# Expert pairs of a decoder step: the next pair's gather inside the down products, a smaller form, another order of pairs

## The reference, cut to what matters

```
logits = h @ w_router + b_router                  # 264 tokens, 8 experts
probs  = softmax(logits)
top_p, top_e = top_k(probs, 2);  top_p /= sum(top_p)
for each token and each of its two experts e:
    out[token] += top_p * ((silu(h @ w_gate[e]) * (h @ w_up[e])) @ w_down[e])
x = x + g_f * out
y = rmsnorm(x, norm_out)
```

## Time and profile before

| | |
|---|---|
| median of three runs | 1342.48 us |
| the profiled execution's own time | 1343.16 us |
| its span, first to last instruction | 1341.3 us |
| PE busy | 1277.4 us (95%) |
| weights and other data read from HBM | 458.94 MB |
| granted TensorE clock, mean | 0.988 |

### The profile page before, as it was taken

How to read it: one execution, slowest core, us unless ns; L and a number is a source line. 1 busy time by engine, 2 the same in 40 slices (tenths; PEclk the granted TensorE clock), 3 DMA queues, 4 the chain that set the end, 5 groups by cost and what they waited for, 6 DMA issues and landing times.

```text
span 1341.3 us, 28791 instructions
## 1 busy us (share of the span) xinstructions
PE 1277.4 (95%) x12903; PEld 746.0 (56%) x12904; DVE 219.8 (16%) x597; ACT 124.5 (9%) x247; POOL 36.1 (3%) x125
## 2 busy tenths in 40 slices
PE   7999999999998699999899999999999999999995
PEld 3777788877885433346565534665343555343553
DVE  0299200000005601010110201002010002010002
ACT  2201310000002310000001000001000001000002
POOL 1000100000003200000000000000000000000000
PEclk9899999999999899999999999999999999999998
DMA  9999575556436299999999899999999999999993
GB/s 334 408 402 387 202 277 201 211 174 231 162 121 251 90 406 417 418 420 423 420 407 352 356 365 423 392 381 420 417 418 420 422 419 417 419 418 418 423 419 121
DMA packets 87885, 462.23 MB, mean 345 GB/s; under 512 B 8747, under 2 KB 12119, under 8 KB 52663
## 3 DMA queue, kind: packets, MB, share of 16 engines
q1 hardware_dynamic: 85937, 456.41, 85.1%
q10 hardware_dynamic: 1814, 3.85, 0.8%
HBM read 458.94 MB, written 2.24 MB: 344 GB/s over the span
## 4 chain that ended last, share of the span: by engine, by line
PE 80%; DMA 13%; DVE 2%; issue 2%; POOL 1%; ACT 1%; SPq 0%; DVEq 0%; ACTq 0%; POOLq 0%
PE bank L1624 36%; PE bank L1389 25%; DMA ring<-in_w_exp_down_dram 13%; PE bank L1646 9%; PE bank L1572 2%; PE bank L1358 2%; PE bank L1678 1%; PE bank L1595 1%; PE bank L1286 1%; POOL ROWS L625 1%; SPq L527 0%; DVE xT L957 0%; ACT MIX L890 0%; PE bank L1516 0%; PE bank L1337 0%
## 5 line engine op out<-in xcount | busy, mean ns | idle before, releaser
L1624 PE MATMUL bank<-ring,HT 128*32 128x512 f32 (+1 forms) x5376 | 510.1, 539 | 3.5 <-DMA ring<-in_w_exp_up_dram 3.5
L1624 PEld LDWEIGHTS bank<-ring,HT 128*32 128x32 f32 x5376 | 189.1, 110 | 312.5 <-issue 298.2
L1389 PE MATMUL bank<-HT,ring 128*128 128x264 f32 x1024 | 234.0, 390 | 2.5 <-POOL HT L619 2.5
L1389 PEld LDWEIGHTS bank<-HT,ring 128*128 128x128 f32 x1024 | 195.4, 192 | 43.6 <-issue 10.3
L1646 PE MATMUL bank<-ring,hid_t 128*32 128x256 f32 x2560 | 149.2, 379 | 2.6 <-DMA ring<-in_w_exp_down_dram 2.6
L1646 PEld LDWEIGHTS bank<-ring,hid_t 128*32 128x32 f32 x2560 | 86.2, 110 | 56.3 <-issue 5.6
L1389 PE MATMUL bank<-BIG,ring 128*128 128x264 f32 x480 | 107.3, 386 | 0.0
L1389 PEld LDWEIGHTS bank<-BIG,ring 128*128 128x128 f32 x480 | 91.1, 190 | 15.5
L1646 PE MATMUL bank<-ring,COND 128*32 128x256 f32 x1568 | 89.6, 380 | 9.9 <-DMA ring<-in_w_exp_down_dram 9.7
L1646 PEld LDWEIGHTS bank<-ring,COND 128*32 128x32 f32 x1568 | 50.2, 110 | 47.8 <-DMA ring<-in_w_exp_down_dram 18.5
L1223 DVE TENSOR_TENSOR hid_t<-bank,hid_t 128x512 f32<-128x512 f32 (+1 forms) x22 | 14.2, 643 | 361.0 <-PE bank L1624 360.3
(11 more groups left out here) (230 smaller groups left out, 527.8 us busy)
## 6 DMA issues: line engine op xcount, KB each, us to landing
ring<-in_w_exp_gate_dram SPq DMA_DIRECT2D x64, 1024.0 KB, 15.1
ring<-in_w_exp_up_dram SPq DMA_DIRECT2D x64, 1024.0 KB, 16.2
ring<-in_w_exp_down_dram SPq DMA_DIRECT2D x64, 1024.0 KB, 24.1
ring<-in_w_ada_dram SPq DMA_DIRECT2D x48, 1024.0 KB, 12.9
ring<-in_w_exp_gate_dram SPq DMA_DIRECT2D x64, 768.0 KB, 16.0
ring<-in_w_exp_up_dram SPq DMA_DIRECT2D x64, 768.0 KB, 14.6
ring<-in_w_exp_down_dram SPq DMA_DIRECT2D x32, 1536.0 KB, 25.2
ring<-in_w_in_dram SPq DMA_DIRECT2D x10, 1024.0 KB, 24.9
```

The costliest lines, as they stand in the source:

```text
L1389: ins = t_.matmul(banks_of[label][:, 0:NT], w[:, k, f * P:(f + 1) * P], src(k0 + k), start=(k0 + k == 0), stop=(k0 + k == k_tiles - 1))
L1624: ins = t_.matmul(bank[GATE_BANKS[role][g]][i * GRP:(i + 1) * GRP, 0:cols], xg[:, k, c0:c0 + GRP], w[:, i, :], start=(k == 0), stop=(k == ...
```

## The change

A fourth form, thin (3 large groups and 1 small), takes the value 0. The ranks of the pairs become (0,6), (1,7), (2,4), (3,5); before they were (0,4), (1,7), (2,5), (3,6). The gather of pair p+1 moves into the down products of pair p: two of its four banks in the large half 0, ahead of the loads 1 and 2, two in the small half 1, ahead of the loads 8 and 10. It uses the banks 3 to 6 and always computes all 224 columns. The first gather stands in front of the loop, and DVE makes its pick matrices and the copy of `pmT` ahead of the flags. The last pair gathers as well, for a pair that does not follow. The store and the spread of `pmT` move from ACT's to POOL's DMA queue.

```diff
-VARIANTS = (("narrow", (3, 2)), ("slim", (5, 1)), ("mid", (5, 2)))
-SLIM = 2
-RANK_AT = (0, 4, 1, 7, 2, 5, 3, 6)
+VARIANTS = (("narrow", (3, 2)), ("slim", (5, 1)), ("thin", (3, 1)), ("mid", (5, 2)))
+THIN, SLIM = 0, 2
+RANK_AT = (0, 6, 1, 7, 2, 4, 3, 5)
...
-GATHER_BANKS = (0, 1, 2, 3)
+GATHER_BANKS = (3, 4, 5, 6)
...
             with nc.body(f"{tag}_not_slim", valid_engines=[kind]):
+                eng.br_eq(form, THIN, on_true=f"{tag}_thin", on_false=f"{tag}_not_thin")
+            with nc.body(f"{tag}_not_thin", valid_engines=[kind]):
                 eng.br_lt(form, SLIM, on_true=f"{tag}_narrow", on_false=f"{tag}_mid")
...
+            pool.wait_ge(on("pmT_ready"), 1)
+            pool.dma_start(pm_rows, pmT[:]).then_inc(on("pm_rows_stored"), 16)
...
             def pair_scalar(p, j, groups):
-                take_batch(p, groups)
...
+                take_batch(p + 1)
                 act.wait_ge(on("large_out_done"), p + 1)
...
+            act.wait_ge(on("new_stored"), 6 * 16)
+            take_batch(0)
             act.wait_ge(on("flags_ready"), 1)
...
             dve.wait_ge(on("pm_ready"), 1)
+            v.tensor_copy(pos_tab[:, :, 0:NE], pm_sorted[:, :, 0:NE])
...
+            dve.wait_ge(on("slots_ready"), 1)
+            pick_matrix(0)
+            empty("turned", v.tensor_copy(pmT[:], wait_bank("turned")[0:2 * NE, 0:NT]))
+            landed("turned")
+            dve.sem_inc(on("pmT_ready"), 1)
             link(v.tensor_tensor(moved[:, 0:2], keys[:].unsqueeze(2).to_broadcast([P, 2, NE, NE]),
...
+            def gather(p, i):
+
+                b = GATHER_BANKS[i]
+                for half in range(2):
+                    d = 2 * i + half
+                    for t in range(3):
+                        ins = t_.matmul(bank[b][:, half * BOTH:(half + 1) * BOTH], h_rows[:, t, d * P:(d + 1) * P],
+                                        pick[t], start=(half == 0 and t == 0), stop=(t == 2), skip_group_check=True)
+                ins.then_inc(on("gathered"), 1)
+
+            pe.wait_ge(on("pick_ready"), 1)
             for bk in range(7):
                 pe.wait_ge(emptied[bk], bank_total[bk])
+            for i in range(len(GATHER_BANKS)):
+                gather(0, i)
             pe.wait_ge(on("flags_ready"), 1)
...
-                gather(p, groups)
...
-                down("large", 0, {4: [("small", 1, g) for g in range(count["small"])]})
-                down("small", 0, {})
+                pe.wait_ge(on("pick_ready"), p + 2)
+                down("large", 0, {4: [("small", 1, g) for g in range(count["small"])]}, {1: 0, 2: 1})
+                down("small", 0, {}, {8: 2, 10: 3})
                 down("large", 1, {})
                 down("small", 1, {})
 
+                pe.wait_ge(on("xg_ready"), p * 4 + 8)
```

More of the change, by code:

```diff
@@ L660, in _ @@
             g.tensor_copy(slot_row, slot_row.bitcast(I32)).then_inc(on("slots_ready"), 1)
+            pool.wait_ge(on("pmT_ready"), 1)
+            pool.dma_start(pm_rows, pmT[:]).then_inc(on("pm_rows_stored"), 16)
+            pool.wait_ge(on("pm_rows_stored"), 16)
+            for i, dst in enumerate((posb, wgtb)):
+                spread = pm_rows[i * NE:(i + 1) * NE, :].rearrange("e n -> (e n)").unsqueeze(0)
+                pool.dma_start(dst.rearrange("p e n -> p (e n)"),
+                              spread.to_broadcast([P, NE * NT])).then_inc(on("tables_spread"), 16)
         @block.scalar
@@ L835, in _, with take_batch @@
             rows(2)
-            def take_batch(p, groups):
-                here = slice(columns_of("large", groups[0] - 1), columns_of("small", groups[1]))
-                for b in GATHER_BANKS:
-                    act.wait_ge(on("gathered"), p * 4 + (b + 1))
-                    src = bank[b][:, 0:2 * BOTH].rearrange("p (t n) -> p t n", t=2)[:, :, here]
-                    a.activation(xg[:, 2 * b:2 * b + 2, here], src, ACT.Copy).then_inc(on("xg_ready"), 1)
+            def take_batch(p):
+                for i, b in enumerate(GATHER_BANKS):
+                    act.wait_ge(on("gathered"), p * 4 + (i + 1))
+                    src = bank[b][:, 0:2 * BOTH].rearrange("p (t n) -> p t n", t=2)
+                    a.activation(xg[:, 2 * i:2 * i + 2, :], src, ACT.Copy).then_inc(on("xg_ready"), 1)
             def pair_scalar(p, j, groups):
-                take_batch(p, groups)
                 for s in range(2):
@@ L1201, in _ @@
             dve.sem_inc(on("pmT_ready"), 1)
+            link(v.tensor_tensor(moved[:, 0:2], keys[:].unsqueeze(2).to_broadcast([P, 2, NE, NE]),
+                                 order.unsqueeze(1).to_broadcast([P, 2, NE, NE]), ALU.mult))
+            link(v.tensor_reduce(sorted_keys[:], moved[:, 0:2], AX_X, ALU.add))
+            v.tensor_copy(excess[:, 0, :], sorted_keys[:, 1, :])
+            link(v.tensor_tensor(excess[:, 1, :], sorted_keys[:, 1, :], caps[:], ALU.subtract))
+            link(v.tensor_reduce(stat[:, 0:1], excess[:, 1, :], AX_X, ALU.max))
+            link(v.tensor_tensor(excess[:], excess[:], fits[:].unsqueeze(1).to_broadcast([P, 2, NE]), ALU.is_gt))
+            link(v.tensor_tensor(excess[:], excess[:], forms[:].unsqueeze(1).to_broadcast([P, 2, NE]), ALU.mult))
+            v.tensor_reduce(flag_f[:, 0:NE].rearrange("p (a j) -> p a j", a=2),
+                            excess[:].rearrange("p a (j r) -> p a j r", r=2), AX_X, ALU.add)
+            v.tensor_copy(flag_f[:, NE:2 * NE], sorted_keys[:, 0, :])
+            link(v.tensor_scalar(flag_f[:, 2 * NE:2 * NE + 1], stat[:, 0:1], 0.0, 1.0, ALU.is_gt, ALU.add))
+            v.tensor_copy(flag[:], flag_f[:]).then_inc(on("flags_ready"), 1)
             dve.wait_ge(on("flags_ready"), 1)
@@ L1553, in _ @@
             fill("turned", ins)
+            ring_flat = ring[:].rearrange("p s n -> p (s n)")
+            L, S = MOST["large"], MOST["small"]
+            def gather(p, i):
[7 more added lines that the diff above has]
+            pe.wait_ge(on("pick_ready"), 1)
             for bk in range(7):
                 pe.wait_ge(emptied[bk], bank_total[bk])
+            for i in range(len(GATHER_BANKS)):
+                gather(0, i)
             pe.wait_ge(on("flags_ready"), 1)
@@ L1558, in _ @@
             pe.wait_ge(emptied[7], bank_total[7])
-            ring_flat = ring[:].rearrange("p s n -> p (s n)")
-            L, S = MOST["large"], MOST["small"]
-            def gather(p, groups):
-                lo, hi = columns_of("large", groups[0] - 1), columns_of("small", groups[1])
-                pe.wait_ge(on("pick_ready"), p + 1)
-                for b in GATHER_BANKS:
-                    pe.wait_ge(on("x_updated"), p * DT + (b + 1))
-                    for i in range(2):
-                        d = 2 * b + i
-                        for t in range(3):
-                            ins = t_.matmul(bank[b][:, i * BOTH + lo:i * BOTH + hi], h_rows[:, t, d * P:(d + 1) * P],
-                                            pick[t][:, lo:hi], start=(i == 0 and t == 0), stop=(t == 2), skip_group_check=True)
-                    ins.then_inc(on("gathered"), 1)
             def pair_tensor(p, j, groups):
@@ L1629, in expand, with down @@
                                 ins.then_inc(on(f"{role}_{kind}_done"), step_of(g, groups, MOST[role]))
-                def down(role, s, turns):
+                def down(role, s, turns, gathers={}):
                     groups, most, half = count[role], MOST[role], HALVES[role][s]
@@ L1636, in down @@
                             turn_hid(*turned)
+                        if u in gathers:
+                            gather(p + 1, gathers[u])
                         parts = DOWN_PARTS[u]
```

29 lines of the change are left out of this document (4 added, 25 removed).

## The result

The changed kernel takes 1354.38 us (median of 4 runs, 1353.03 to 1354.6), the kernel before beside it 1342.57 (1340.36 to 1344.75): ratio 1.0086, interval 1.0068 to 1.0104. It is 11.8 us slower; the forecast was 1344.7, with 1348.5 as the upper end. Its profiled execution has a span of 1352.6 us where that of before has 1341.3, so 11.3 us have to be found in the two traces.

What follows compares the result with a forecast made beforehand. One path sets the end: flags, stream through pair 0, PE into pair 1's large down product, stream to last landing, PE's tail. +1.3 us at the last landing and +0.9 in the tail give +2.2: 1344.7 us, range 1340.2 to 1348.5.

Steps and rivals of the forecast that it cites:

- the gap at the turn from pair 0 to pair 1: PE's idle time before pair 1, behind the loop's branch: claimed to stay at 2.6 us without the gather.
- The path: Flags, stream through pair 0, PE to pair 1's large down product, stream to last landing, PE's tail; +2.2 us in all.
- The rival with the gap: Behind pair 0 the turn takes 1.2 us and the clock stays up: -1.4 and -1.9, 1341.4 us; chance 0.15.
- The last load and the place: End of pair 0: 16 fewer matmuls behind the last landing, -0.87, and 16 fewer in the place, -0.94 us.
- the rival at 0.25: The clock falls in pair 0's small down product: +2.8 us, bounds +0.9 and +4.6, 1347.5; chance 0.25.
- Flags: Behind the router, picks and pmT copy ahead of the flag chain on DVE delay flags and stream: +1.83 us.
- that costs nothing: Pair 0's first expansion starts near 474.6, not 472.8; cost 0, since the ring's first free slot moves with the stream.
- The gather that goes: Between pairs 0 and 1 the gather disappears, half clock stays: -7.8 us, bounds -7.8 and -9.7.
- The gather that comes: A gather for pair 2 enters pair 1's down products, all of it paid: +9.1 us, bounds +7.8 and +9.7.
- The tail: The last pair's extra gather of 9.1 us, partly absorbed by PE's waits: +0.9 us, between 0 and +2.7.
- The gather in pair 1 is free: Rival: the ring's last full moment lies before pair 1's down products: -9.1, 1335.6 us; chance 0.07.
- The new form isn't used: Rival: pair 0 still runs five groups: +1.8, 1346.5 us; chance 0.03.

Runs made afterwards that it cites:

- e1: The changed kernel with the thin body put ahead of the slim one in the program, same instructions: 1348.83 us, ratio 1.0046.
- e7: The kernel before with only the thin form and new ranks, thin body written second so that slim follows it: 1339.92 us, ratio 0.9978.
- e14: e7 with 48 slots of never-run padding on PE behind the thin body, slim body meant to start at slot 30: 1350.93 us, ratio 1.0046.
- e16: e7 with the never-run mid body and padding between thin and slim, slim still at slot 237: 1356.49 us, ratio 1.0091.
- e17: The changed kernel with the bodies in the order in which they run (thin, slim, narrow, mid): 1352.97 us, ratio 1.0072.
- e10: e5 with one more gather, its result unread, in the down products of the slim body (pair 1): 1351.43 us, ratio 1.0057.
- e6: The kernel before with only the thin form and new ranks, bodies ordered narrow, slim, thin, mid: 1347.6 us, ratio 1.0029.
- e5: e7 with only the thin body gathering ahead; the others gather at their top, the slim one not at all: 1336.36 us, ratio 0.995.
- e13: e5 with never-run padding on PE behind the thin body, so slim starts at slot 237 and not 30: 1341.86 us, ratio 0.9989.
- e18: e5 with the bodies in the order in which they run (thin, slim, narrow, mid): 1341.82 us, ratio 0.9988.
- e9: e5 with one more gather, its result unread, in the down products of the narrow body (pairs 2 and 3): 1343.05 us, ratio 1.0005.
- e11: e5 with the slim body ahead of the thin one in the program: 1343.37 us, ratio 1.0002.
- e3: The changed kernel with the four insertions of each gather moved to the second small down product: 1353.84 us, ratio 1.0077.
- e4: The changed kernel with the flag chain ahead of the picks on DVE again: 1357.17 us, ratio 1.0109.
- e15: The changed kernel with never-run padding on PE before the slim body, which starts at slot 237 and not 158: 1364.49 us, ratio 1.0149.
- e12: e7 with 300 never-run register moves written between the thin and slim bodies, possibly absent from the program: 1340.35 us, ratio 0.998.

## Why the prediction was wrong

The step that failed is the gap at the turn from pair 0 to pair 1: the prediction kept it at 2.6 us, and it was 6.80. The path held otherwise, and several other terms were each a little low.

- *"The gap is not the gather's: with the gather gone the first expansion stands behind the same branch"*, the gap kept at 2.6 us. This step failed. The branch is the same, but what stands behind it is not: before, the body of pair 1 followed that of pair 0 in the program (narrow, slim); now thin stands behind slim. Measured 6.80, so +4.16. e1 and e7 take it away by order alone, e14 and e16 bring it back by place alone. The rival with the gap had it shrinking; no rival had it growing, though the prediction named the branch as what is late next.
- *The last load and the place*, -1.81: it was -1.07 (5.52 us from the last load's start to the place's end, 6.59 before), since the clock fell at 660.5. That was the rival at 0.25, and its condition came true, which the prediction names as a sign of being wrong: the granted clock reads 0.50 in 660 to 665, before the place of pair 0. Its price of +2.8, with 0.9 as the lower bound, was too high: the loads hide most of it, and the place ran at the upper level again (3.84 us for 64 matmuls), so +0.74. PE worked 1.07 us in 2.49, 43%; the prediction's 1 us in 2.5 is 40%, not 38. The rule of the Trainium skill that the prediction names (TensorE: Matmul & The Clock Gate, "What's actually happening"), that recent activity alone releases the throttle, pointed this way; the trace agrees with it.
- *Flags* +1.83: 2.0. With the router's own 0.34 and 0.12 of drift, the last load starts 2.48 later than before. Pair 0's first expansion was to start near 474.6 and started at 477.84, behind 5.91 us ended by issue: the same kind of stop as at the turn. e17, without it, starts the place of pair 0 1.3 us earlier, so "that costs nothing" was not quite right.
- *The gather that goes* -7.8: it frees 9.67 us of PE time, but the half clock stays, as forecast, and now slows expansions (0.50 in 677.8 to 680). From 677.77 to 907.09, the end of the large down product, are 229.3 us; before, 681.87 to 899.10, 217.2.
- *The gather that comes* +9.1: of these +12.1 us it is 9.9, four times 2.47 in the chain, and some 2 are the clock.

At that point the sum is 2.48 - 1.07 + 4.16 - 9.67 + 12.09 = +8.0, forecast +1.3; the stream is behind by 8.76 at the last pair's first down load. Of the missing 6.7 us the jump is 4.2, the clock 0.74 and 0.3 more in pair 1, the gather 0.8, flags and drift 0.65. The 0.8 between 8.0 and 8.76 is not traced. So the jump is under half of the 9.1 us by which the span missed the forecast; without it the forecast would still have been low.

- *The tail* +0.9: 1.6 at the place, within the bounds given, and 1.0 behind it, where a stop ended by issue splits the final transposes.
- *Rivals.* "The gather in pair 1 is free": excluded, 9.0 us in e10 and 331 GB/s in the changed kernel. "The new form isn't used": excluded, 20 groups.
- *What it should have shown.* The stall of 20 to 22 us, "less at its beginning and more in its down products", reads 22.2 us in the two stretches of the earlier trace rows, and is 26.1 with what stands behind 903. Whoever looks at the two stretches alone takes it for right and misses that pair 1 started late: 677.77 measured, 674.1 by the forecast's terms. The way from pair 0's last load to pair 1's first expansion became 6.6 us shorter (12.3, before 18.9), not 9.6.
- *A slip of reading.* The slice with 90 GB/s is 13 by the count that the prediction uses elsewhere (21 to 26), not 14; nothing hangs on it.

The pieces of the change: the form with its ranks is worth -3 us in the best place tried and +4 in the one it was given; the rest of the change, gather ahead and late flags, costs 6.8 more on top (from e6 to the changed kernel; 8.9 from e7 to e1). Pair 1's gather holds the ring (9.0 us in e10); that the last pair's costs 1.6 us at the end is read from the trace alone. e5 keeps only pair 0's, which falls into waits.

What stays open: which neighbouring bodies are there in time. With the slim body next in the program and in the block in which its predecessor ends, the idle time was 0.94 in e7 (slot 237) and 5.34 in e5 (slot 30) and e13 (slot 237); in e14 the 48 slots push it into the next block, 6.82. For the other runs in which the slim body follows directly no slots are on record: 0.94 (e1), 0.94 (e17), 0.81 (e18), 2.96 (e9), 5.44 (e10). Second stops came after 6, 7, 31, 53 or 61 expansion matmuls. The turn from pair 1 to 2, to the narrow body, which stands right behind the loop's head in all but e17 and e18, cost 0.7 to 5.7 us. Each body's last branch carries a hint (`branch_hint`, L460) that no run varied. No rule tried here gives all of these.

## What to carry to other kernels

In a loop with several long bodies, an added, moved or lengthened body is priced with its jumps: 1 to 10 us of idle time a turn in this kernel, on the path wherever the turn is not followed by a wait for data. Look in the trace for idle time ended by issue at each turn and for the instruction queue's packets ahead of it, and compare variants of a kernel only with these rows side by side: e7 and e14 differ by 48 slots that never run and by some 10 us. Work moved into waiting time pays only in the pair that waits, so move it there alone (e5), not in the common body.

## What the runs showed of the hardware

- Instruction fetch: packets of 16 KB on a queue of their own. In the changed kernel, e13 and e17 PE goes on 2 to 5 us after one has come, while the weight stream runs at some 420 GB/s. PE's idle time at the turn to a slim body that is not at hand was 6.80, 6.82, 6.85, 6.85, 6.87, 6.88 and 7.15 us in seven kernels (changed, e14, e6, e11, e16, e3, e4) and 10.36 in e15; without a stop it was 0.81 to 0.96 (e18, e1, e7, e17, e12).
- The granted clock fell to 0.50 by 660.5 us in the changed kernel, behind two loads with 1.07 us of work in 2.49 each, and in e7 by 659.45 behind loads of the same kind. In the kernel before, with 1.93 us of work in 2.48, it read 1.00.
